# Retention in one chunk of 128 tokens per tile in place of two of 64, and the next tile's loads issued ahead of the residual stores

## What is computed

```python
idx = jnp.arange(CHUNK)                       # CHUNK = 64
rel = idx[:, None] - idx[None, :]
decay_in = where(rel >= 0, exp(log_gamma * max(rel, 0)), 0.0)
q_decay = exp(log_gamma * (idx + 1))
k_decay = exp(log_gamma * (CHUNK - 1 - idx))
chunk_decay = exp(log_gamma * CHUNK)
scores = einsum('nbhcd,nbhmd->nbhcm', qc, kc) * decay_in
inner = einsum('nbhcm,nbhme->nbhce', scores, vc)
def step(R, inp):
    cross = einsum('bhcd,bhde->bhce', q_c, R) * q_decay
    R = R * chunk_decay + einsum('bhmd,bhme->bhde', k_c * k_decay, v_c)
    return R, cross
```

## Time and profile before

| | |
|---|---|
| median of 3 runs | 1731.52 us (1729.84 to 1734.58) |
| the profiled execution's own time | 1733.71 us |
| its span, first to last instruction | 1731.9 us |
| mean granted clock of PE, share of full speed | 0.912 |
| PE busy | 1479.7 us, 85% of the span |
| DVE busy | 951.0 us, 55% |
| ACT busy | 697.0 us, 40% |
| mean DMA rate | 212 GB/s |

### The profile page before, as it was taken

How to read it: one execution, slowest core, us unless ns; L and a number is a source line. 1 busy time by engine, 2 the same in 40 slices (tenths; PEclk the granted TensorE clock), 3 DMA queues, 4 the chain that set the end, 5 groups by cost and what they waited for, 6 DMA issues and landing times. The chain is left out here.

```text
span 1731.9 us, 32895 instructions
## 1 busy us (share of the span) xinstructions
PE 1479.7 (85%) x14419; PEld 1275.8 (74%) x14419; DVE 951.0 (55%) x1014; ACT 697.0 (40%) x669; POOL 632.9 (37%) x215
## 2 busy tenths in 40 slices
PE   5999999999698889888889830799999999999940
PEld 4989999999696667667668620688888888888830
DVE  5455664442144354354355341678787787778726
ACT  4442342223121121121121100677777878777712
POOL 1001110000000000000000003899999999999934
PEclk9999999999888898898998965899999999999975
DMA  5133445343392231222230178699999999999856
GB/s 182 50 119 126 148 136 171 90 130 86 110 356 95 104 96 60 104 70 86 105 97 35 38 50 293 220 401 414 414 414 413 415 413 415 413 415 414 316 196 252
DMA packets 188628, 366.59 MB, mean 212 GB/s; under 512 B 17169, under 2 KB 76864, under 8 KB 187472
## 3 DMA queue, kind: packets, MB, share of 16 engines
q1 hardware_dynamic: 175328, 318.69, 51.8%
q0 software_dynamic: 7424, 25.18, 3.8%
q10 hardware_dynamic: 5760, 20.97, 3.0%
HBM read 295.81 MB, written 69.01 MB: 211 GB/s over the span
## 5 line engine op out<-in xcount | busy, mean ns | idle before, releaser
L1057 PE MATMUL ps<-u_hi,w_hi 128*128 128x352 f32 (+1 forms) x720 | 239.6, 333 | 6.9 <-DVE u_lo L708 6.9
L1057 PE MATMUL ps<-u_lo,w_hi 128*128 128x352 f32 (+1 forms) x720 | 235.3, 327 | 0.0
L1057 PE MATMUL ps<-u_hi,w_lo 128*128 128x352 f32 (+1 forms) x720 | 234.3, 325 | 0.0
L2398 POOL TENSOR_TENSOR down_lo<-down_raw,down_hi 128x1024 fp32r<-128x1024 f32 x32 | 178.6, 5581 | 31.4 <-ACT down_hi L2443 31.4
L2398 POOL TENSOR_TENSOR gate_lo<-gate_raw,gate_hi 128x1024 fp32r<-128x1024 f32 x32 | 177.3, 5540 | 6.5 <-ACT gate_hi L2443 6.5
L2526 DVE TENSOR_TENSOR down_lo<-down_raw,down_hi 128x3072 fp32r<-128x3072 f32 x32 | 109.4, 3420 | 97.1 <-ACT down_hi L2443 97.1
L2398 POOL TENSOR_TENSOR up_lo<-up_raw,up_hi 128x1024 fp32r<-128x1024 f32 x32 | 154.8, 4838 | 1.6 <-ACT up_hi L2443 1.0
L1057 PEld LDWEIGHTS ps<-u_hi,w_hi 128*128 128x128 f32 x720 | 138.9, 193 | 13.9 <-issue 10.6
L1057 PEld LDWEIGHTS ps<-u_lo,w_hi 128*128 128x128 f32 x720 | 138.8, 193 | 0.0
L1057 PEld LDWEIGHTS ps<-u_hi,w_lo 128*128 128x128 f32 x720 | 138.8, 193 | 0.0
L2443 ACT ACTIVATE gate_hi<-gate_raw 128x4096 fp32r<-128x4096 f32 x32 | 116.5, 3641 | 53.0 <-SPq L2341 53.0
(11 more groups left out here) (379 smaller groups left out, 3190.5 us busy)
## 6 DMA issues: line engine op xcount, KB each, us to landing
gate_raw<-in_moe_w_gate SPq DMA_DIRECT2D x32, 2048.0 KB, 12.4
up_raw<-in_moe_w_up SPq DMA_DIRECT2D x32, 2048.0 KB, 14.2
down_raw<-in_moe_w_down SPq DMA_DIRECT2D x32, 2048.0 KB, 12.8
tm_rows<-tm_stage SPq DMA_DIRECT2D x32, 512.0 KB, 3.3
y_slots<-y_out ACTq DMA_DIRECT2D x32, 512.0 KB, 6.8
w_raw<-in_w_in SPq DMA_DIRECT2D x30, 512.0 KB, 3.7
tm<-tm_rows SPq DMA_DIRECT2D x8, 1792.0 KB, 8.7
fm<-fm_rows SPq DMA_DIRECT2D x8, 1024.0 KB, 6.7
```

The source lines that it names most:

```text
L1057: mm = pe.matmul(z_of(n, r_), w[n % 3][:, k_, :], a[:, k_, c0:c1], start=(k_ == 0 and i == 0), stop=(k_ == KD - 1 and i == 2))
L2398: pool.tensor_tensor(lo[e % 2][:, cut:, :], raw[e % 2][:, cut:, :], hi[:, cut:, :].bitcast(F32), ALU.subtract).then_inc(sem(f"{name}_lo2_r ...
```

## The change

Scores, inner and cross are computed for 128 tokens at once, so a mask of 512 columns takes the place of one of 256, and the memory is advanced once per tile. `ret_second` and the DVE operations `memory_second` and `memory_last` are gone. On SP, the three loads of tile t + 1 now stand together behind the waits for `rz_t_ready`, `mixed_b_ready` and `y0_done` of n, q and kr first, then v to rg, then a to r, and the stores of h2(n) and u2(n) come behind them.

```diff
-    ("ret_mask", HB * C), ("q_decay", HB), ("k_decay", HB), ("r_decay", HB), ("k_decay_meta", HB),
+    ("ret_mask", HB * P), ("q_decay", HB), ("k_decay", HB), ("r_decay", HB), ("k_decay_meta", HB),
...
                     if t + 1 < NT:
                         sp.wait_ge(sem("rz_t_ready"), n)
+                        sp.wait_ge(sem("mixed_b_ready"), n)
                         sp.wait_ge(sem("y0_done"), n)
+                        load_fm(t + 1, "q", "kr")
+                        load_tm(t + 1, "v", "rg")
                         load_fm(t + 1, "a", "r")
                     store_h2(n)
                     load_h(t)
                     store_u2(n)
-                    if t + 1 < NT:
-                        sp.wait_ge(sem("mixed_b_ready"), n)
-                        load_fm(t + 1, "q", "kr")
-                        load_tm(t + 1, "v", "rg")
...
-                    tt(s_t[:], ps[:, 3, 0:HB * C], cst("ret_mask"), ALU.mult, "s_t_ready")
+                    tt(s_t[:], ps[:, 3, :], cst("ret_mask"), ALU.mult, "s_t_ready")
...
-                def memory_second(t):
-                    dve.wait_ge(sem("memory1_ready"), t)
-                    tt(heads(memory_d[:], HB), heads(memory[1][:], HB), per_head(cst("r_decay"), HB), ALU.mult, "memory_d1")
-
-                def memory_last(t):
-                    dve.wait_ge(sem("memory_d1"), t)
-                    dve.wait_ge(sem("kv1_done"), t)
-                    tt(memory[0][:], memory_d[:], ps[:, 7, :], ALU.add, "memory0_ready")
+                def memory_next(t):
+
+                    dve.wait_ge(sem("memory_d"), t)
+                    dve.wait_ge(sem("kv_done"), t)
+                    tt(memory[t % 2][:], memory_d[:], ps[:, 4, :], ALU.add, "memory_ready")
...
                 def ret_scores(t):
...
-                    for c in range(2):
-                        for h in range(HB):
-                            f = slice(h * P + c * C, h * P + (c + 1) * C)
-                            mm = pe.matmul(ps[c * C:(c + 1) * C, 3, h * C:(h + 1) * C], kr_t[:, f], q_t[:, f], start=True, stop=True)
+                    for h in range(HB):
+                        f = slice(h * P, (h + 1) * P)
+                        mm = pe.matmul(ps[:, 3, f], kr_t[:, f], q_t[:, f], start=True, stop=True)
...
+                def ret_keys(t):
                     pe.wait_ge(sem(f"tm_v_loaded{t % 2}"), 16 * ((t + 1) // 2))
-                    key_values(4, t, 0).then_inc(sem("kv0_done"), 1)
+                    for h in range(HB):
+                        f = slice(h * P, (h + 1) * P)
+                        mm = pe.matmul(ps[:, 4, f], toks(t, "kd")[:, f], toks(t, "rv")[:, f], start=True, stop=True)
+                    mm.then_inc(sem("kv_done"), 1)
...
-                def ret_second(t):
-                    pe.wait_ge(sem("in_s_ready"), t)
-                    key_values(7, t, 1).then_inc(sem("kv1_done"), 1)
...
                     advance(4, m_t[:, 0, :], state[0]).then_inc(sem("s1_done"), 1)
                     if t + 1 < NT:
-                        ret_second(t + 1)
                         pe.wait_ge(sem("y_ret_ready"), t + 1)
```

More of the change, by code:

```diff
@@ L108, in shape_constants @@
     scale = HEAD_B ** -0.5
-    rel = t - s
+    rel = q - p
     c["ret_mask"] = np.concatenate([np.where(rel >= 0, np.exp(g * np.maximum(rel, 0)), 0.0) * scale for g in lg], 1)
-    c["q_decay"] = np.exp(lg[None, :] * (s + 1))
-    c["k_decay"] = np.exp(lg[None, :] * (C - 1 - s)) * scale
+    c["q_decay"] = np.exp(lg[None, :] * (p + 1))
+    c["k_decay"] = np.exp(lg[None, :] * (P - 1 - p)) * scale
     c["k_decay_meta"] = np.exp(lg[None, :] * (N_META - 1 - p % N_META)) * scale
-    c["r_decay"] = np.exp(lg * C)[None, :] + np.zeros((P, 1))
+    c["r_decay"] = np.exp(lg * P)[None, :] + np.zeros((P, 1))
     c["group_prio"] = np.arange(N_GROUPS, 0, -1)[None, :] + np.zeros((P, 1))
@@ L1246, in mix @@
         state, kept = [sb(f"state{i}", DA // 2) for i in range(2)], [sb(f"kept{i}", DA // 2) for i in range(2)]
-        s_t, in_s, y_ret, ret_sq, crossed = sb("s_t", HB * C), sb("in_s", DB), sb("y_ret", DB), sb("ret_sq", DB), sb("crossed", DB)
+        s_t, in_s, y_ret, ret_sq, crossed = sb("s_t", HB * P), sb("in_s", DB), sb("y_ret", DB), sb("ret_sq", DB), sb("crossed", DB)
         memory, memory_d = [sb(f"memory{i}", DB) for i in range(2)], sb("memory_d", DB)
@@ L1552, in scores, with memory_decay @@
                     dve.wait_ge(sem("scores_done"), t)
-                    tt(s_t[:], ps[:, 3, 0:HB * C], cst("ret_mask"), ALU.mult, "s_t_ready")
-                def memory_first(t):
+                    tt(s_t[:], ps[:, 3, :], cst("ret_mask"), ALU.mult, "s_t_ready")
+                def memory_decay(t):
                     if t == 1:
@@ L1668, in body @@
                         scores(1)
-                        memory_first(1)
-                        memory_second(1)
+                        memory_decay(1)
+                        memory_next(1)
                     dve.wait_ge(sem("inv_4"), t)
@@ L1677, in body @@
                         b_rows(1)
-                        memory_last(1)
                         b_centre(1)
@@ L1695, in body @@
                     if t + 1 < NT:
-                        memory_first(t + 1)
-                        memory_second(t + 1)
+                        memory_decay(t + 1)
+                        memory_next(t + 1)
                     dve.wait_ge(sem("z0_a_ready"), t)
@@ L1710, in body @@
                         b_rows(t + 1)
-                        memory_last(t + 1)
                     state_last(t)
@@ L1862, in turn_y @@
                     if n < NTX:
-                        pe.wait_ge(sem("memory0_ready"), n + 1)
+                        pe.wait_ge(sem("in_s_ready"), n + 1)
                     turn4(7, y).then_inc(sem("y_turned"), 1)
@@ L1886, in route @@
                     mm.then_inc(sem("router_done"), 1)
-                def key_values(bank, t, c):
-                    p_ = slice(c * C, (c + 1) * C)
-                    for h in range(HB):
-                        f = slice(h * P, (h + 1) * P)
-                        mm = pe.matmul(ps[:, bank, f], toks(t, "kd")[p_, f], toks(t, "rv")[p_, f], start=True, stop=True)
-                    return mm
                 def ret_scores(t):
@@ L1909, in ret_inner @@
                 def ret_inner(t):
                     pe.wait_ge(sem("s_t_ready"), t)
[L1911 to L1915, removed]
+                    for h in range(HB):
+                        f = slice(h * P, (h + 1) * P)
+                        mm = pe.matmul(ps[:, 7, f], s_t[:, f], toks(t, "rv")[:, f], start=True, stop=True)
@@ L1916, in ret_inner @@
                     mm.then_inc(sem("inner_done"), 1)
                 def ret_cross(t):
[L1919 to L1923, removed]
+                    if t == 1:
+                        pe.wait_ge(sem("m_memory_ready"), 1)
+                    else:
+                        pe.wait_ge(sem("memory_ready"), t - 1)
@@ L1924, in ret_cross @@
+                    for h in range(HB):
+                        f = slice(h * P, (h + 1) * P)
+                        mm = pe.matmul(ps[:, 6, f], feat(t, "q")[:, f], memory[(t - 1) % 2][:, f], start=True, stop=True)
                     mm.then_inc(sem("cross_done"), 1)
-                def ret_second(t):
-                    pe.wait_ge(sem("in_s_ready"), t)
-                    key_values(7, t, 1).then_inc(sem("kv1_done"), 1)
                 def turn_ret(t, bank):
@@ L1997, in body @@
                         ret_scores(1)
-                        ret_first(1)
+                        ret_keys(1)
                     pe.wait_ge(sem("inv_4"), t)
@@ L2009, in body @@
                         ret_cross(1)
-                        ret_second(1)
                     pe.wait_ge(sem("inv_ready"), t)
@@ L2014, in body @@
                         pe.wait_ge(sem("s_t_ready"), 1)
-                        pe.wait_ge(sem("memory1_ready"), 1)
+                        pe.wait_ge(sem("memory_ready"), 1)
                     chunks(3, [(lo, inv)]).then_inc(sem("x_t_done"), 1)
@@ L2030, in body @@
                     if t + 1 < NT:
-                        ret_first(t + 1)
+                        ret_keys(t + 1)
                     if n:
@@ L2034, in body @@
                     else:
-                        pe.wait_ge(sem("memory0_ready"), 1)
+                        pe.wait_ge(sem("in_s_ready"), 1)
                         turn_ret(1, 7)
@@ L2047, in body @@
                         ret_inner(t + 1)
-                        pe.wait_ge(sem("memory1_ready"), t + 1)
+                        pe.wait_ge(sem("memory_ready"), t + 1)
                     pe.wait_ge(sem("w_m_ready"), t)
```

8 lines of the change are left out of this document (2 added, 6 removed).

## The result

| | before | after |
|---|---|---|
| median | 1730.68 us (4 runs, 1723.11 to 1734.58) | 1667.17 us (4 runs, 1660.0 to 1673.91) |
| ratio to before | | 0.9638, 95% interval 0.9584 to 0.9691 |
| profiled execution | 1733.7 us | 1669.1 us |
| mean granted clock | 0.912 | 0.929 |

The change makes the kernel 63.5 us faster. The prediction was 1684 us with a range of 1664 to 1708.

The account below looks back on a forecast made before the run. PE was held by late loads queued behind u2's store, then ran at half clock. 63.2 + 2.5 + 1.5 - 3.0 - 0.4 - 9.5 - 6.6 = 47.7 us off the median 1731.5 gave 1684 us, range 1664 to 1708.

Parts of the forecast that it names:

- The loads: Stretch from x2 chunks to `ret_inner`, bodies 2 to 7: earlier loads cut 112.4 us to 8.2 each, saving 63.2 us.
- Cross: `ret_cross` on PE: 16 instructions become 8, 1.51 us becomes 1.09, saving 2.5 us over six bodies.
- Body 1: In body 1, removing `ret_second` gives 1.1 us and cross 0.4, together 1.5 us.
- Inner: `ret_inner` on PE: full-width instructions can't lie beside to_features; -0.4 to +0.5 us a body, taken as -3.0 us.
- What is given back: Two losses of unknown size: the clock behind the y_ret wait, -9.5 us, and PE's issue stalls, -6.6 us.
- The clock behind y_ret: PE's longer wait for y_ret lowers its clock behind it: 1.9 us in five of six bodies, -9.5 us.
- the stall: Early in bodies, PE's instructions arrive late behind loads at `y0_done`: two more issue waits at 3.3 us, -6.6 us.
- Constants: At the start, the larger table of constants loads 128 KB more: between nothing and 0.7 us, taken as -0.4 us.
- merging gains nothing: Rival: two half chunks already overlap in PE's array, so cross still takes 1.5 us; 1688 us, chance 0.08.
- the stalls don't grow: Rival: PE's issue stalls add nothing while the clock term stands, 6.6 us less; 1677 us, chance 0.10.
- Nothing is given back: Rival: neither PE's clock nor its stalls get worse; 1668 us, or 1658 with the three stalls gone; chance 0.17.
- slower: Rival: at each body's start PE's instructions wait until all 3.25 MB land, 74 us against 63.8; 1742 us, chance 0.03.

Follow-up runs that it names:

- Experiment 1: The kernel before with only SP's new order of loads, the retention still in two chunks: 1671.4 us against 1726.2, ratio 0.9706.
- experiments 6 and 8: Kernel of experiment 4 with PE waiting ahead of `ret_scores` for made-up GpSimd operations, two in 6, five in 8: 1683.5 and 1699.8 us.
- experiment 4: The changed kernel with SP also waiting for `inv4_done` before the three loads: 1656.1 us, ratio 0.9609 to the kernel before.
- experiment 2: The changed kernel with SP's order of before, so the merged retention alone: 1715.9 us against 1726.2 for the kernel before, ratio 0.9944.
- experiments 4, 5 and 12: 5 and 12: the changed kernel with `crossed` and `y_ret` ahead of state and kept on DVE, loads behind `inv4_done`: 1640.2 and 1637.8 us; experiment 4 has its own line.
- experiment 3: The changed kernel with `crossed` and `y_ret` moved ahead of state and kept on DVE: 1645.6 us, ratio 0.9539 to the kernel before.

## Why the prediction was right, and where it was off

- **The loads** (63.2 us): right, 65.1. The stretch was put together as 8.2 us from rows and is 7.95; each of its groups lies within 0.12 us of its row. Experiment 1 shows that the order of SP's queue does this by itself, and experiments 6 and 8 that idle time with the clock behind it is what such a wait costs, with no load running.
- **Cross** (2.5): right, 2.5 (29.1 to 26.5), and the wait for y_ret grew to 2.37 us as said. So the 1.09 us that `ret_second` had taken on PE gave nothing in bodies 2 to 7.
- **Body 1** (1.5): 1.9.
- **Inner** (-3.0): wrong, nothing. Inner to cross is 4.18 us in every one of the six bodies, before and after. Between my ends of -0.4 and +0.5 I took the loss; the merged form neither gained nor lost. The rows of before in body 6 show why: the instructions of the second half start at 858.22, while those of the first half still start until 858.54, and the last of them starts at 859.04, behind the start of to_features at 858.72. The rule of the Trainium skill ("TensorE: Matmul & The Clock Gate", Part 3) that half chunks on different row groups overlap fits this place, and not cross, where full contraction rows were used before and 16 half-wide instructions took 1.51 us.
- **What is given back** (-16.1): the term that was mis-sized. It was 6.1 in y0 to x2 and 1.5 in body 8's, 7.6. The clock behind y_ret is its real part: I took five of six at 1.9, 9.5; experiment 4, which has that and no stalls, shows four of six at 1.7, 7.0, and body 8 had another 1.5. The step that failed is the stall, -6.6. I took the three issue waits of before as staying and added two at 3.3 us. The number of waits came out, five of over half a microsecond in place of three, but three of them are short (0.7 to 1.0): 7.6 us of waits for 5.7. And what y0 to x2 loses beyond the clock behind y_ret did not grow: 229.8 - 208.9 - 7.0 = 13.9 us in the changed kernel against 223.7 - 208.9 = 14.8 in the one before. My sign of it, more than three issue waits ahead of the cross matmuls, failed too: there are two. The other, issue waits of over 3 us a body, came true in body 7 alone, 3.2 us.

  The two halves of the change, run alone, show what the sum had left out:

  | kernel | y0 to x2 | issue waits over 0.4 us, bodies 2 to 7 |
  |---|---|---|
  | before | 223.7 | 5.7 us: bodies 2, 4, 6 |
  | loads alone (1) | 226.4 | 7.3 us: bodies 2, 4, 5, 6, 7 |
  | retention alone (2) | 222.3 | 3.3 us: bodies 4, 7 |
  | both (changed) | 229.8 | 7.6 us: bodies 3, 4, 5, 6, 7 |

  With the retention merged, the new order of the loads costs 7.5 us in y0 to x2, near my 6.6. But merging takes stalls away: it is 1.4 us lower although its longer y_ret wait costs some 7 of clock, so by this estimate some 8 us of the old stalls went with it. That the loads hold up PE's instructions, and that more of them do it more, was right; that the old stalls would stay where they were was not. These are differences of single traces, good to some 4 us.
- **Constants** (-0.4): not to be seen; the start of `mix` differs by more than that from run to run.

Taken together, the span fell by 64.6 us where the sum had 47.7, 16.9 more. Of that, 8.5 are given back less than I took (7.5 stalls, 1.0 clock), 3.0 inner, 1.9 the stretch, 0.4 body 1, and 3.7 the start of `mix` with the constants, which moves by itself from run to run; this makes 17.5, and 0.6 is lost at the tail. So the measured time lies 17 us under the forecast, near the low end of the range, with the paths right and nearly every size on the careful side. Of the rivals, "merging gains nothing" held for inner alone, and "the stalls don't grow", at 1677, held in its net effect. "Nothing is given back", at 1668, has the nearest number by luck: 7.6 us were given back, and inner, the stretch and the start of `mix` made up for them. The rival "slower" has a slip in its sum: 18.7 less 6.6 less 8.2 is 3.9 and not 4.2, so its case is 1740 us; no argument hangs on it. The Trainium skill ("Runtime: NRT & Kernel Launch", "Instruction fetch mechanics") says that instructions are fetched ahead and the cost is mostly hidden. In experiments 4, 5 and 12 the trace agrees for bodies 2 to 7; in body 1 it does not, where the same block brings 1.2, 4.8 and 0.9 us, nor with a load issued at `y0_done`, with waits up to 3.6 us.

Why the same bodies are hit each time follows from the blocks of 127 records. A tile has 1088 matmul records with the old retention, so after two tiles (2176) the end of a block is back at nearly the same matmul (17 blocks are 2158): bodies 2, 4 and 6. With the merged retention it has 1056, and three tiles are 3168 for 25 blocks of 3173: bodies 4 and 7. Experiments 1 and 2 separate this from the loads. The retention alone moves the waits ahead of the cross matmuls from bodies 2, 4 and 6 to 4 and 7, and the loads alone leave them where they were.

What stays open: why the clock comes back sooner in the stretches of the merged retention alone (experiment 2) with its DMA waits in place, and by what way a load makes an instruction packet start late.

## What to carry to other kernels

Issue a load where its buffer comes free, and not behind a store that waits for something else on the same queue: here one queue's order held PE up for 6.7 us per tile, and with the clock behind the idle time the price was 11. When an operation is removed, look what its time had covered: `ret_second` gave nothing until the DVE chain behind it was reordered (experiment 3), which was worth 17 to 22 us in the changed kernel. What that reordering alone gives in the kernel before was not run. Place big loads beside long instructions, and not where PE runs through hundreds of short ones.

## What was not expected of the hardware

Ahead of `ret_scores` the granted clock punished short waits in steps: 1.1 us idle never, 2.3 us in five of six bodies (1.5 us each), 5.1 us in six of six (2.5 us each). Length alone does not decide it: the issue wait of 1.42 us in body 6 of before, in another place of the body, was followed by a piece at half clock. And a load under way can starve PE of instructions for up to 3.6 us. The rows of body 4 of the changed kernel show the pattern, the three loads on SP's queue and, 4 us behind the first of them (645.66 less 1.92), the start of a wait that no engine ended; the instruction packet that it was for had landed at 644.17:

```profile
639.66 0.37 SPq L1301 DMA_DIRECT2D fm<-fm_rows  x1
...
640.39 0.33 SPq L1305 DMA_DIRECT2D tm<-tm_rows  x1
...
640.77 0.43 SPq L1301 DMA_DIRECT2D fm<-fm_rows  x1
...
645.66 1.29 PE L1744 MATMUL ps<-fm 64*64 64x64 f32 x26 [1.92 <-issue]
```
